# A two-layer transformer trunk on one core: half-by-half stage ends, routing tables built on GpSimd, and small expert items loaded by 2048-column rows

## What is computed

```python
h = h + mla(rms_norm(h, g0), ...)                 # 8 heads, low-rank K/V, output product o @ w_o
h = h + swiglu(rms_norm(h, g1), w_gate_up, w_down)    # dense, hidden width 2816
kv = rms_norm(h, g2) @ kv_shared_w
h = h + stick_breaking(rms_norm(h, g3), w_q, w_o, k, v)   # ends with o @ w_o too
probs = softmax(x @ router)                       # x = rms_norm(h, g4), 8 experts
top_p, top_i = top_k(probs, 2)                    # gates = top_p / sum(top_p)
for e in range(8):
    y = y + gates[:, e:e + 1] * swiglu(x, w_gate_up[e], w_down[e])   # hidden width 2816
h = rms_norm(h + y, g5)
```

## Time and profile before

| | us |
|---|---|
| median of three runs | 1124.07 |
| the profiled execution | 1122.33 |
| its span, first to last instruction | 1120.5 |
| TensorE busy | 1080.2 (96%) |
| VectorE busy | 625.7 (56%) |
| ScalarE busy | 523.5 (47%) |
| GpSimd busy | 23.1 (2%) |
| granted TensorE clock, mean | 0.996 |
| moved by DMA | 343.47 MB, mean 307 GB/s |

### The profile page before, as it was taken

The page is one execution under the profiler, slowest core; times in us unless marked ns, Lnnn a source line. Parts: engine busy times, 40 slices in busy tenths (PEclk is TensorE's granted clock), DMA queues, the critical chain, the costliest instruction groups (busy, mean ns, idle before and its releaser), DMA issues.

```text
span 1120.5 us, 15883 instructions
## 1 busy us (share of the span) xinstructions
PE 1080.2 (96%) x5832; PEld 808.0 (72%) x5832; DVE 625.7 (56%) x711; ACT 523.5 (47%) x578; POOL 23.1 (2%) x94
## 2 busy tenths in 40 slices
PE   9998999999999999999998999998999998999994
PEld 9887888888899887887355888355888355888451
DVE  6866455455644558895106896106896105897102
ACT  6565444344445644775014775014775005776001
POOL 1100000000000000000000000000000000000000
PEclk9999999999999999999999999999999999999998
DMA  9933556555454333998999999999999999999994
GB/s 343 364 121 113 186 175 203 170 191 202 151 188 150 113 113 125 381 362 296 359 418 408 403 418 409 391 417 409 404 415 410 395 414 410 405 414 409 398 412 195
DMA packets 110935, 343.47 MB, mean 307 GB/s; under 512 B 11613, under 2 KB 38282, under 8 KB 100618
## 3 DMA queue, kind: packets, MB, share of 16 engines
q1 hardware_dynamic: 110714, 341.93, 80.5%
q10 hardware_dynamic: 144, 0.52, 0.1%
HBM read 341.37 MB, written 1.05 MB: 306 GB/s over the span
## 4 chain that ended last, share of the span: by engine, by line
PE 79%; DMA 7%; DVE 7%; SPq 3%; issue 2%; ACT 1%; POOL 0%; POOLq 0%; DVEq 0%; ACTq 0%
PE ps L1495 20%; PE ps L1490 19%; PE ps L1492 19%; PE ps L1491 19%; DMA raw<-moe_w_gate_up_dram 5%; SPq L372 2%; DMA raw<-moe_w_down_dram 2%; DVE wlo L970 1%; PE ps L1838 1%; DVE wlo L957 1%; DVE wlo L959 1%; DVE h L1224 1%; ACT whi L565 1%; DVE h L1152 1%; DMA raw<-mla_w_down_dram 1%
## 5 line engine op out<-in xcount | busy, mean ns | idle before, releaser
L565 ACT ACTIVATE whi<-raw 128x2048 fp32r<-128x2048 f32 (+2 forms) x203 | 341.6, 1688 | 235.9 <-PE ps L1492 218.9
L970 DVE TENSOR_TENSOR wlo<-raw,whi 128x2048 fp32r<-128x2048 f32 x151 | 345.4, 2293 | 115.1 <-ACT whi L565 114.4
L1490 PE MATMUL ps<-whi,xhi 128*128 128x512 f32 (+3 forms) x688 | 263.5, 383 | 11.5 <-DVE wlo L970 10.5
L1492 PE MATMUL ps<-wlo,xhi 128*128 128x512 f32 (+3 forms) x688 | 259.5, 377 | 0.0
L1491 PE MATMUL ps<-whi,xlo 128*128 128x512 f32 (+3 forms) x688 | 259.0, 376 | 0.0
L1490 PEld LDWEIGHTS ps<-whi,xhi 128*128 128x128 f32 x688 | 129.5, 188 | 38.9 <-DVE wlo L970 9.0
L1495 PE MATMUL ps<-raw,xs 128*64 128x512 f32 (+2 forms) x1024 | 155.0, 461 | 0.0
L1492 PEld LDWEIGHTS ps<-wlo,xhi 128*128 128x128 f32 x688 | 129.3, 188 | 23.8
L1491 PEld LDWEIGHTS ps<-whi,xlo 128*128 128x128 f32 x688 | 129.5, 188 | 22.4
L1495 PEld LDWEIGHTS ps<-raw,xs 128*64 128x64 f32 x1024 | 68.3, 137 | 81.7 <-issue 71.5
L1490 PE MATMUL ps<-whi,hhi 128*128 128x512 f32 x264 | 105.9, 401 | 0.0
(11 more groups left out here) (299 smaller groups left out, 972.8 us busy)
## 6 DMA issues: line engine op xcount, KB each, us to landing
raw<-moe_w_gate_up_dram SPq DMA_DIRECT2D x256, 512.0 KB, 14.0
raw<-moe_w_down_dram SPq DMA_DIRECT2D x80, 1024.0 KB, 17.8
raw<-moe_w_gate_up_dram SPq DMA_DIRECT2D x96, 384.0 KB, 9.5
raw<-ffn_w_gate_up_dram SPq DMA_DIRECT2D x44, 512.0 KB, 5.0
raw<-ffn_w_down_dram SPq DMA_DIRECT2D x22, 512.0 KB, 4.2
raw<-kv_shared_w_dram SPq DMA_DIRECT2D x16, 512.0 KB, 4.2
raw<-moe_w_gate_up_dram SPq DMA_DIRECT2D x32, 256.0 KB, 9.6
raw<-moe_w_down_dram SPq DMA_DIRECT2D x16, 512.0 KB, 18.3
```

The lines of the kernel that those rows point to most:

```text
L565: return nc.scalar.activation(o, i, ACT.Copy, scale=scale)
L970: V.tensor_tensor(wlo[:, s, :].rearrange("p a w -> p (a w)"), raw[:, (hh // 2) % RAW, :], whi[:, s, :].bitcast(F32).rearrange("p a w -> p ...
L1490: pe.matmul(o, a_hi, b_hi, start=start, stop=False, skip_group_check=True)
L1492: return pe.matmul(o, a_hi, b_lo, start=False, stop=stop, skip_group_check=True)
```

## The change

Three things change, with what hangs on them.

**Half by half ends.** The last heads of both attention outputs run first for tokens 0 to 127, then for 128 to 255 (the last two heads of the first attention, the last four of the second). The additions to `h`, the transposes and the splits follow by halves. The first products of the dense layer take all four weight halves for c = 0, then for c = 1. The router is now the stationary side, padded to 32 columns in four column groups, and an extra small product (`collect`) sums and turns the result. The first item's `sel` comes from a shorter test (`first_msk`: fewer than two experts beat expert 0), before the second pick. Several `keep_clock` products are dropped.

**Tables on GpSimd.** The list of items, `pm_tab` and `g_tab` are built by 60 GpSimd operations, each waiting for the one before, after two copies by VectorE (`counted`). They stand in GpSimd's program ahead of the first `scatter_weights`. VectorE's `item_gates` and `choose` move in a big item from x = 14 to x = 25, behind a wait for `tables_ready`; in a small one ahead of the gates.

**Small items.** A unit of the first 16 is 2048 gate columns (0 to 7) or 2048 up columns (8 to 15) of a row chunk, loaded by two transfers of 64 rows by 8 KB. The gates of both 512-wide groups follow unit 15, their transposes units 17 and 19; the last groups move to PSUM banks 5 and 7.

```diff
-            def item_unit(x, w_gu, w_dn):
+            def item_unit(x, w_gu, w_dn, kind):
                 u = U_MOE + x
-                if x < GU:
+                if kind == "small" and x < 16:
+                    a, k = x // 8, x % 8
+                    for n in range(2):
+                        rows_of = slice(n * SMALL, (n + 1) * SMALL)
+                        sp_eng.dma_start(raw[rows_of, u % RAW, :], w_gu[k * P + n * SMALL:k * P + (n + 1) * SMALL, a * FF:a * FF + 2048]
+                                         ).then_inc(landed[u % RAW], 16)
+                elif x < GU:
...
+            pool.wait_ge(counted, 2)
+            step(G.tensor_scalar(key[:, :], cnt[:, :], float(N_EXP), None, ALU.mult))
...
+            G.tensor_copy(item_expert[:, :], tf[:, :]).then_inc(items_ready, 1)
+            G.tensor_scalar(final_i[:, :], extra[:, 2:3], float(PAIRS - 1), None, ALU.add).then_inc(items_ready, 1)
...
+            step(sum8(pm_tab[:, :, :, :].rearrange("p i q c -> p (q c) i").unsqueeze(3), lambda a, b: each[:, :, :, a:b]))
+            pool.wait_ge(counted, 3)
...
+            sum8(g_tab[:, :, :].rearrange("p i c -> p c i").unsqueeze(3), lambda a, b: each[:, 0:TC, :, a:b]).then_inc(tables_ready, 1)
...
-                    if x == 14:
+                    if x == 25:
+                        dve.wait_ge(tables_ready, 1)
                         item_gates(g)
                         choose(g + 1, following)
...
             gathered_low(0)
-            split_low(H_SBO + RING + 7)
+            for m in range(6, 8):
+                split_low(H_SBO + RING + m)
+            dve.wait_ge(pos_done, 2)
+            V.tensor_copy(posn[:, :, :].rearrange("p c e -> p (c e)"), ps[:, 5, 288:304]).then_inc(counted, 1)
+            V.tensor_copy(cnt[:, :], ps[:, 5, 304:312]).then_inc(counted, 1)
...
+            for c in range(TC):
+                for k in range(HEADS - 2, HEADS):
+                    if c == 0:
+                        pe.wait_ge(o_lo, k + 1)
+                        pe.wait_ge(lo_made, H_WO + k + 1)
+                    last = tokens_of(c, k, H_WO + k, ((4, 5), (6, 7)))
+                    if c == 1:
+                        last.then_inc(used, 1)
+                        transpose_half(0, k - HEADS + 2)
+                if c == 0:
+                    last.then_inc(wo_half, 1)
...
-                            last = mm(ps[n * SMALL:(n + 1) * SMALL, 2 * (x // 8) + a, :], xs[:, k, :], r[:, w], k == 0, k == KD - 1)
+                            last = mm(ps[n * SMALL:(n + 1) * SMALL, 2 * j + x // 8, :], xs[:, k, :], r[:, w], k == 0, k == KD - 1)
...
+            for c in range(TC):
+                for k in range(KD):
+                    if k % 4 == 0:
+                        pe.wait_ge(xhi_ready[3], 2 * c + k // 4 + 1)
+                    j = k % 4
+                    last = mm(ps[32 * j:32 * (j + 1), LG_BANKS[c], 0:P], router_w[:, k, :], xr[:, k, c * P:(c + 1) * P], k < 4, k >= 4)
+                last.then_inc(lg_done, 1)
+                keep_clock(2, 4)
```

More of the change, by code:

```diff
@@ L708, in _, with x_half_high @@
                 split_high(22 + hd)
-            for hh in range(30, 32):
-                split_high(hh)
+            def x_half_high(q):
+                c, b = q // 2, q % 2
+                act.wait_ge(x_tr[1], q + 1)
+                for k in range(4 * b, 4 * b + 4):
+                    copy(xhi[:, k, c * P:(c + 1) * P], ps[:, X_BANKS[1][q], k % 4 * P:(k % 4 + 1) * P],
+                         scale=gcol[:, G_FFN0 + k:G_FFN0 + k + 1]).then_inc(xhi_ready[1], 1)
+            x_half_high(0)
+            x_half_high(1)
+            split_high(30)
+            split_high(31)
             def ffn(x):
@@ L822, in small @@
                     silu(j)
+                for j in range(2):
                     hidden(j)
@@ L1277, in small @@
                     choose(g + 1, following)
-                for j in range(1, SMALL_GROUPS):
+                for j in range(SMALL_GROUPS):
                     gate(j)
@@ L1463, in _ @@
+            for x in range(3, 5):
+                split_low_unit(H_MOE + 2 * x)
             V.memset(table_scratch[:, :], 0.0).then_inc(h_ready[4], 4)
@@ L1642, in _, with transpose_half @@
             value_features(0)
+            def transpose_half(c, b):
+                pe.wait_ge(h_ready[1], 2 * c + b + 1)
+                for k in range(4 * b, 4 * b + 4):
+                    last = pe.transpose(ps[:, X_BANKS[1][2 * c + b], k % 4 * P:(k % 4 + 1) * P], h[:, c, k * P:(k + 1) * P], ident[:, :])
+                last.then_inc(x_tr[1], 1)
             def scores(hd):
@@ new lines, in _ @@
+            suffix_sums(1)
+            sb_outputs(1)
+            for c in range(TC):
+                for k in range(4, 8):
+                    if c == 0:
+                        pe.wait_ge(so_lo, k + 1)
+                        pe.wait_ge(lo_made, H_SBO + k + 1)
+                    last = tokens_of(c, k, H_SBO + k, ((0, 1), (2, 3)))
+                    if c == 1:
+                        last.then_inc(used, 1)
+                if c == 0:
+                    last.then_inc(so_half, 1)
+            for b in range(4):
+                c = b // 2
+                pe.wait_ge(h_ready[3], 2 if c == 0 else b + 1)
+                for k in range(b % 2 * 4, b % 2 * 4 + 4):
+                    last = pe.transpose(ps[:, X_BANKS[3][b], k % 4 * P:(k % 4 + 1) * P], h[:, c, k * P:(k + 1) * P], ident[:, :])
+                last.then_inc(x_tr[3], 1)
@@ new lines, in _ @@
+            pe.wait_ge(router_ready, 1)
+            for c in range(TC):
+                for k in range(KD):
[5 more added lines that the diff above has]
+                keep_clock(2, 4)
+            for c in range(TC):
+                pe.wait_ge(xhi_ready[3], 4 + c + 1)
+                last = mm(ps[:, 2, c * N_EXP:(c + 1) * N_EXP], lgT[:, c * P:(c + 1) * P], collect[:, :], c == 0, True)
```

355 lines of the change are left out of this document (197 added, 158 removed).

## The result

The changed kernel takes 1233.42 us (median of four runs, 1221.51 to 1235.76) against 1123.6 us for the kernel before beside it: ratio 1.0952, 95% interval 1.0878 to 1.1027. The forecast was 1113 us, faster. The change is 110 us slower.

The account below looks back on a forecast made before the run. TensorE sets the pace to about 540 us, then TensorE and loads alternate within each pair of items. Terms -2.0 - 8.7 + 1 - 1 = -10.7 us give 1111.6 profiled, forecast 1113 us (1109 to 1117).

Parts of the forecast that it names:

- Small items' units: Small items' first 16 units: 8 KB rows land faster, only about four units count; -1 us over four items, at most -5.
- rival 1: Small items' first 16 units: transfers to half the partitions run at half rate; 1270 us in turn, 1187 half overlapped; chance 0.17.
- estimate of 77 us: Small items' first 16 units: 16.8 MB by the skill's page at 218 GB/s; not followed for the forecast.
- threshold: Rate of small items' first 16 units below which half rate decides: 367 GB/s, or 4.7 us more per item.
- First attention's end: Between first attention and dense layer: work by halves shortens the 4.13 us wait; gain 2.0 us, at least 1, at most 2.2.
- Second attention's end: From second attention's last product (T) to first item's unit 4: T+23.5 instead of T+32.2; gain 8.7 us, 7.5 to 9.5.
- Tables on GpSimd: First big item: 60 GpSimd operations beside VectorE's splits, ready at T+89, just fitting; +1 us, between 0 and +5.
- rival 3: Small items: loads bound throughout, so all first 16 units count, -5.2 us instead of -1; 1109 us, chance 0.10.
- rival 4: Both attention ends: halves wait for each other or the clock falls, half of 10.7 us is gone; 1118 us, chance 0.09.
- rival 2: First big item's tables: GpSimd locked out, one operation beside each split, 34 left when VectorE arrives; 1121 us, chance 0.14.
- The sum: Whole kernel: -2.0 - 8.7 + 1 - 1 = -10.7 us, 1111.6 on the profiled execution, 1113 us as median.
- wrong if that pair is longer than 172: Sign in the changed profile: a pair of items, big and small, should still take 170 us; over 172 refutes the prediction.

Follow-up runs that it names:

- the kernel by columns: Changed kernel, but each of a small item's first 16 units comes by two transfers of 128 rows of 1024 columns: 1112.12 us, again 1111.84.
- the one-transfer run: Changed kernel, but each of a small item's first 16 units comes by one transfer of 128 rows of 8 KB: 1113.37 us, ratio 0.9904.
- twelve stages: No computation: expert rows loaded into 16 buffers, one stage per choice of partitions, row length, order or queue; 208 to 424 GB/s.
- the run with whole ends: The kernel by columns, but both attention ends wait for whole products and the first end's half 0 transposes follow its last product: 1118.44 us.

## Why the prediction was wrong

- **Small items' units, -1 us: here it failed.** The step took the rates of 128-partition rows (410 and 423 GB/s) for transfers to 64 partitions, of which no row existed. It named the right doubt (rival 1), gave its price, and then set it aside with the argument that some 13 transfers for both halves were under way at a time. That argument is what the runs refute: 0-63 and 64-127 in turn give 225 GB/s alone, and 222 to 297 in the kernels, against 410. Many transfers queued is not many transfers moving to both halves at once. Term by term: -1 forecast, +121 measured.
- **Rival 1, 1187 or 1270 us.** The time was 1233, between its two ends: an item lost 30 us in the mean (1233.4 - 1112.1 = 121.3 over four), not 41, since the halves in turn run at 234 GB/s, not at half of 410. The room was there, as the first item lost some 20 us and not 30, but in the changed kernel the last item lost some 38; with the rows of the kernel before split, one item ran at up to 297 GB/s and lost only 20. The prediction's estimate of 77 us for 16.8 MB by the page leaves out the 6% named beside it; with it 73 us, and at the 234 GB/s measured 72. Its threshold (a rate under 367 GB/s) was passed by far. A chance of 0.17 was too low for a case that the Trainium skill's page stated outright, with a measured +6%, and against which no row stood; the range left it out wholly.
- **First attention's end, -2.0 us (1 to 2.2).** The second attention's last product ends 2.5 us earlier in the kernel by columns (408.38 against 410.9), with 0.74 us, filled by four transposes, between last and first product. A little better than the range: the 16 transposes cost 1.8 us there too, in four groups (0.74 and three times 0.36), but the wait of 0.2 did not come. 4.13 - 1.8 = 2.3, and 0.2 more was gained ahead of the last product.
- **Second attention's end, -8.7 us.** Right: logits at T+5.0 (forecast T+5.3), gather at T+7.7 (T+7.9), unit 0 at T+12.15 (T+12.3), and no wait of TensorE from 422 to 432, so unit 4 at about T+23.3 (T+23.5). The clock stayed at 1.00 with 20 filler products less.
- **Tables on GpSimd, +1 us (0 to 5).** Right in the rate (60 operations in 70 us, 1.17 us each; forecast 72 slots of 1 us) and in the end (494.3; forecast T+89, 497), and the fit was as narrow as said: 2.1 us. It cost 0. Of the 60, 23 were held for the length of a split or two. The list came at 473.3 (T+65; forecast T+67). Twelve more steps are past the edge, and there the working had one term too few: the clock after the wait.
- **Loads bound throughout (rival 3).** Falls with the one-transfer run. The ends did what they say (rival 4 falls), GpSimd was not locked out (rival 2 falls, with the tables ready 2.1 us early).
- **The sum.** Without the units' transfer the sum -10.7 us, 1111.6, stands against 1111.37 in the profiled execution of the kernel by columns: the parts that had rows were priced well, the one without a row was 11 times the rest. Some of the closeness is luck: the tables' +1 and the longer rows' -1 were both nothing and cancel. Beside the kernel before, the gain of the kernel by columns is 11.8 and 13.6 us (ratios 0.9895 and 0.9879), a little more than 10.7.

The claim "wrong if that pair is longer than 172" was the one that came true, with 190 to 208.

## What to carry to other kernels

Split a load over columns or over whole row chunks, never into partitions 0-63 and 64-127: that moved 210 to 297 GB/s here against 410, with every order, row length and queue tried. Judge loads by GB/s and not by the DMA share, which read 1.02 at 410 and at 211 alike. When a term of a sum has no row, and its bounds are 1 us and 120 us apart, the sum is not a forecast until that term is measured alone; if only a written rule prices it, the argument against the rule needs a row of its own.

The version that keeps the half ends, the tables on GpSimd and the new unit, with two transfers of 128 rows, beats both kernels: 1112 us, 0.9895 and 0.9879 of the kernel before, on two chips.

## What the runs showed of the hardware

- Transfers to partitions 32-95 alone run at 416 GB/s, to 0-63 alone at 211; two queues of different engines for the two halves reach 262, and quarters in the two orders tried 242 and 245.
- Transfers to 0-63 and 64-127 in turn have no fixed rate within a kernel: 222 to 297 GB/s in windows of 10 us, from the same queue.
- The share of busy time of the DMA engines doesn't fall when the partitions limit them: 1.00 to 1.03 in all twelve stages.
- A wait of 2.96 us of TensorE cost about 3.4 us more, by some 6.8 us at 1.2 GHz behind it (3.4 / 0.50). Filled with unused products the clock stayed at 2.4 GHz. In the run with whole ends, waits of 1.38 and 1.78 us, with 1.09 us of transposes between them, were also followed by windows at 0.50.
- A small GpSimd operation beside VectorE's splits is often held for the length of a split (2.36 us at 485.54, where 0.19 to 0.22 are usual). In a chain of 60 this befell 23, so that the chain ran at 1.17 us an operation:

```profile
485.54 2.36 POOL L635 TENSOR_TENSOR rt_oh<-rt_oh,rt_m 128x16 f32<-128x16 f32 x1
487.98 0.22 POOL L636 TENSOR_TENSOR rt_oh<-rt_oh,rt_m 128x16 f32<-128x16 f32 x1
```
